# Last step of the conv FFNs in three chunks instead of four, and the order of work at the norm transitions

## What is computed

```python
def rmsnorm(x, g):
    y = xf * lax.rsqrt(jnp.mean(xf * xf, axis=-1, keepdims=True) + EPS)
    return (y * g.astype(jnp.float32)).astype(x.dtype)

def conv_gated_ffn(h, w_up, conv_w, conv_b, w_down):      # w_up 1024 x 2*2752, w_down 2752 x 1024
    u = h @ w_up
    u = lax.conv_general_dilated(u, conv_w[:, None, :], ..., feature_group_count=C) + conv_b
    gate, val = jnp.split(u, 2, axis=-1)
    return (jax.nn.silu(gate) * val) @ w_down
```

## Time and profile before

| | |
|---|---|
| median of 3 executions | 1830.35 us (1830.26 to 1830.57) |
| the profiled execution | 1831.45 us, span 1829.7 us |
| mean granted clock of TensorE | 0.992 |
| PE, matmuls | 1786.2 us, 98% of the span, 14408 instructions |
| DVE, ACT | 1248.0 us (68%), 999.3 us (55%) |
| weights read | 302.48 MB, 166 GB/s over the span; 16 DMA engines about half busy |

### The profile page before, as it was taken

How to read it: one execution, slowest core, us unless ns; L and a number is a source line. 1 busy time by engine, 2 the same in 40 slices (tenths; PEclk the granted TensorE clock), 3 DMA queues, 4 the chain that set the end, 5 groups by cost and what they waited for, 6 DMA issues and landing times.

```text
span 1829.7 us, 35759 instructions
## 1 busy us (share of the span) xinstructions
PE 1786.2 (98%) x14408; PEld 1737.5 (95%) x14408; DVE 1248.0 (68%) x1799; ACT 999.3 (55%) x1493; POOL 76.4 (4%) x125
## 2 busy tenths in 40 slices
PE   7999999999999999999999999998999999999998
PEld 6999999999999998999999999998999999989997
DVE  6667877765787776787776687786655675656554
ACT  4666555654655566655566665565444645445443
POOL 1000000011000004000000000000200010000000
PEclk8999999999999999999999999998999999999999
DMA  8344655534465545465554456554555453535552
GB/s 276 123 155 143 205 182 167 173 127 127 151 208 181 169 162 162 141 206 184 166 168 145 136 177 206 191 159 139 186 183 183 155 181 127 173 105 195 184 183 92
DMA packets 229466, 305.31 MB, mean 167 GB/s; under 512 B 4985, under 2 KB 204203, under 8 KB 229310
## 3 DMA queue, kind: packets, MB, share of 16 engines
q1 hardware_dynamic: 228150, 299.28, 50.8%
q0 software_dynamic: 1088, 4.22, 0.7%
q10 hardware_dynamic: 104, 0.07, 0.0%
HBM read 302.48 MB, written 1.07 MB: 166 GB/s over the span
## 4 chain that ended last, share of the span: by engine, by line
PE 79%; DVE 9%; ACT 7%; issue 3%; DMA 1%; ACTq 0%; DVEq 0%
PE ps L957 25%; PE ps L958 24%; PE ps L959 24%; DVE sb_w_lo L1463 4%; ACT sb_w_hi L802 3%; DVE sb_work L1814 2%; PE ps L1114 1%; DVE sb_work L1800 1%; DMA sb_raw<-in_da_w_qkv 1%; PE ps L1134 0%; ACT sb_a_hi L842 0%; ACT sb_work L912 0%; PE ps L1201 0%; DVE sb_y L1538 0%; ACT sb_hh L934 0%
## 5 line engine op out<-in xcount | busy, mean ns | idle before, releaser
L957 PE MATMUL ps<-sb_a_hi,sb_w_hi 128*128 128x256 f32 x3152 | 905.8, 287 | 20.4 <-DVE sb_w_lo L1463 10.8
L1463 DVE TENSOR_TENSOR sb_w_lo<-sb_raw,sb_w_hi 128x2048 fp32r<-128x2048 f32 x284 | 649.6, 2291 | 393.8 <-ACT sb_w_hi L802 393.7
L958 PE MATMUL ps<-sb_a_lo,sb_w_hi 128*128 128x256 f32 x3152 | 894.7, 284 | 0.0
L959 PE MATMUL ps<-sb_a_hi,sb_w_lo 128*128 128x256 f32 x3152 | 894.5, 284 | 0.0
L802 ACT ACTIVATE sb_w_hi<-sb_raw 128x2048 fp32r<-128x2048 f32 x284 | 540.0, 1906 | 290.7 <-PE ps L959 270.1
L957 PEld LDWEIGHTS ps<-sb_a_hi,sb_w_hi 128*128 128x128 f32 x3152 | 607.1, 193 | 31.9 <-DVE sb_w_lo L1463 12.4
L958 PEld LDWEIGHTS ps<-sb_a_lo,sb_w_hi 128*128 128x128 f32 x3152 | 607.3, 193 | 0.8
L959 PEld LDWEIGHTS ps<-sb_a_hi,sb_w_lo 128*128 128x128 f32 x3152 | 607.3, 193 | 0.0
L957 PE MATMUL ps<-sb_hh,sb_w_hi 128*128 128x256 f32 (+1 forms) x912 | 257.7, 283 | 4.6 <-DVE sb_w_lo L1463 3.4
L958 PE MATMUL ps<-sb_hl,sb_w_hi 128*128 128x256 f32 (+1 forms) x912 | 256.8, 282 | 0.0
L959 PE MATMUL ps<-sb_hh,sb_w_lo 128*128 128x256 f32 (+1 forms) x912 | 256.6, 281 | 0.0
(11 more groups left out here) (211 smaller groups left out, 1426.9 us busy)
## 6 DMA issues: line engine op xcount, KB each, us to landing
sb_raw<-in_ffn_w_up SPq DMA_DIRECT2D x102, 1024.0 KB, 5.3
sb_raw<-in_ffn_w_down SPq DMA_DIRECT2D x62, 1024.0 KB, 4.9
sb_raw<-in_da_w_qkv SPq DMA_DIRECT2D x24, 1024.0 KB, 5.2
sb_raw<-in_ffn_w_gate SPq DMA_DIRECT2D x22, 1024.0 KB, 5.3
sb_raw<-in_w_o SPq DMA_DIRECT2D x16, 1024.0 KB, 4.9
sb_raw<-in_sb_w_qkv SPq DMA_DIRECT2D x12, 1024.0 KB, 5.1
sb_raw<-in_xa_wkv SPq DMA_DIRECT2D x8, 1024.0 KB, 5.4
sb_raw<-in_w_in SPq DMA_DIRECT2D x8, 1024.0 KB, 5.3
```

The source lines that it names most:

```text
L957: pe.matmul(o, hi1, hi2, start=start, stop=False, skip_group_check=True)
L958: pe.matmul(o, hi1, lo2, start=False, stop=False, skip_group_check=True)
L959: return pe.matmul(o, lo1, hi2, start=False, stop=stop, skip_group_check=True)
L1463: dve.tensor_tensor(w_lo[:, a % RING, :], raw[:, a % RING, :], w_hi[:, a % RING, :].bitcast(F32), ALU.subtract).then_inc(lo_ready, 1)
```

## The change

1. **Last step of the conv FFNs** (`packed`). Chunk 0 becomes 128 gate and 128 value channels. The 64 that are left share one chunk: their gate and value columns stand side by side in one matmul, gate in PSUM partitions 0 to 63 and value in 64 to 127. The first up block holds 128 gate and 128 value columns, the second 64 and 64. Both are loaded by two DMAs each, and SP waits for the first to land before it issues the second. `take` of the second chunk is two instructions of 64 partitions; it writes partitions 64 to 127, and all later work of that chunk, the down product too, uses these (`rows`).
2. **First step** of all FFNs but the last one: part 0 slice by slice, then part 1 whole.
3. **Bridges, ACT:** w_hi of n+3 stands behind the first pair of hi copies, and the four squares of the next norm behind all hi copies.
4. **First bridge:** the sum of the memory's squares moves on DVE to the FFN before, right behind `mem_lo`; w_lo of block 34 moves behind the four additions of `finish`. On PE both `square_total`s stand together in the first block (j = 1, k = 5).

```diff
         if ph["mem_turned"]:
             stat(ph["mem_turned"])
+            ph["tree"], ph["mem_turned"]["tree"] = ph["mem_turned"]["tree"], ph["tree"]
...
+        def packed(ph, s0):
+            return s0 == NSTEP - 1 and ph["F"] == F1
+        def rows(ph, s0, c):
+            return slice(HD, P) if packed(ph, s0) and c else slice(0, P)
...
                     def up(s0, s, ph=ph):
                         for part in range(2):
...
+                            if packed(ph, s0):
+                                n, first = (P, HD)[part], 2 * P * s0 + P * part
+                                halves = [io[w][l][:, h * F1 + first:h * F1 + first + n].rearrange("(k p) n -> p k n", p=P)
+                                          for h in range(2)]
+                                wait_block(sp, b - RING)
+                                sp.dma_start(slot(b, KC)[:, :, n:2 * n], halves[1]).then_inc(s_half_in, 16)
+                                sp.wait_ge(s_half_in, 16 * (2 * ph["index"] + part + 1))
+                                load(b, s, slot(b, KC)[:, :, 0:n], halves[0])
+                                continue
...
                     for i in range(4):
-                        prep_pair(ph["then"], i)
-                    if ph["blocks"]:
-                        split(ph["n"] + 3)
+                        prep_hi(ph["then"], i)
+                        if i == 0 and ph["blocks"]:
+                            split(ph["n"] + 3)
+                    for i in range(4):
+                        square_pair(x[:, 2 * i:2 * i + 2, :], i)
...
-                            if (i, j, k) == (0, 1, 1):
+                            if (i, j, k) == (0, 1, 5 if ph["mem_turned"] else 1):
                                 square_total(ph["stat"], ph["tree"], ph["bank"])
-                            if ph["mem_turned"] and (i, j, k) == (1, 1, 3):
-                                mem = ph["mem_turned"]
-                                square_total(mem["stat"], mem["tree"], 4 + (ph["bank"] - 3) % 4, sq_mem)
+                                if ph["mem_turned"]:
+                                    mem = ph["mem_turned"]
+                                    square_total(mem["stat"], mem["tree"], 4 + (ph["bank"] - 3) % 4, sq_mem)
...
                 def up(s0, s):
                     for part in range(2):
                         wait_block(pe, up_block(ph, s0, part), s)
-                        for c in range(2):
+                        for i in range(2 * KC):
+                            first = s0 == 0 and part == 0
+                            c, k = (i % 2, i // 2) if first else (i // KC, i % KC)
...
+                            if first and c == 0:
+                                wait_slice(k)
+                            ins = up_product(s0, part, c, k)
...
+                    if s0 == 0:
+                        square_total(ph["stat"], tree_of[ph["stat"]])
+                def packed_up(s0):
+                    for part in range(2):
+                        b, u = up_block(ph, s0, part), ph["u"] + 2 * s0 + part
+                        wait_block(pe, b)
+                        pe.wait_ge(u_free, u - 3)
+                        wh, wl = weights(b, KC)
+                        for h in range(2 - part):
+                            cs = slice(h * P, (h + 1) * P)
+                            for k in range(KC):
+                                ins = product(UB[u % 4][:, h * T:(h + 1) * T], wh[:, k, cs], wl[:, k, cs],
+                                              a_hi[a][:, k, :], a_lo[a][:, k, :], k == 0 and h == 0, k == KC - 1)
...
-                first_up()
+                if ph["dst"] == "tok":
+                    both_first_ups()
+                else:
+                    up(0, 0)
...
-                if ph["mem_turned"]:
-                    dve.wait_ge(sq_mem_ready, 4)
-                    square_sum(sq_mem)
...
                     def take(c):
-                        if c == 0:
+                        if c == 0 and packed(ph, s0):
+                            dve.wait_ge(blocks_done, b + 1)
+                        elif c == 0:
                             dve.wait_ge(half_done, ph["hd"] + s0 + 1 + s)
...
+                        if packed(ph, s0) and c:
+                            ps = rows(ph, s0, c)
+                            for h in range(2):
+                                ins = dve.tensor_tensor(us[ps, c, h, :], UB[u % 4][h * HD:(h + 1) * HD, 0:T], r_all[ps, 0, :],
+                                                        ALU.mult)
...
                 def down(s0, s):
-                    if s0 < NSTEP - 1:
+                    if s0 < NSTEP - 2 or s0 == NSTEP - 2 and "mem" not in ph:
                         split(down_block(ph, s0) + 3, s)
                     if s0 == NSTEP - 3:
                         hidden_lo(NSTEP - 1, 0)
                         if "mem" in ph:
                             mem_lo(ph["mem"]["fill"])
+                            square_sum(sq_mem)
...
                 if ph["dst"] == "x":
                     chunk_pairs(ph, finish)
+                if "mem" in ph:
+                    split(down_block(ph, NSTEP - 2) + 3)
```

More of the change, by code:

```diff
@@ L503, in down @@
                     def down(s0, s, ph=ph):
-                        n = cols(ph, s0)
                         w, l = ph["down"]
                         b = down_block(ph, s0)
-                        src = io[w][l][bass.ds(2 * P * s0 + 2 * P * s, 2 * n), :]
-                        load(b, s, slot(b, 2)[0:n, :, :], src.rearrange("(k p) n -> p k n", p=n))
+                        if packed(ph, s0):
+                            row0 = io[w][l][2 * P * s0:2 * P * s0 + P, :]
+                            src = bass.AP(row0.tensor, row0.offset, [[D, P], [HD * D, 2], [1, D]])
+                            return load(b, s, slot(b, 2), src)
+                        src = io[w][l][bass.ds(2 * P * s0 + 2 * P * s, 2 * P), :]
+                        load(b, s, slot(b, 2), src.rearrange("(k p) n -> p k n", p=P))
                     ffn_steps(sp, up, down)
@@ L926, in up @@
                                 act.wait_ge(hid_ready, f - 1 + 2 * s)
-                                src = us[0:n, c, 0, :]
-                            act.activation(sil[0:n, c, :], src, ACT.Silu).then_inc(sil_ready, 1)
+                                src = us[ps, c, 0, :]
+                            act.activation(sil[ps, c, :], src, ACT.Silu).then_inc(sil_ready, 1)
                         for c in range(2):
@@ L933, in up @@
                             act.wait_ge(hid_ready, ph["f"] + 2 * s0 + c + 1 + 2 * s)
-                            act.activation(hh[0:n, 2 * (s0 % 2) + c, :], hid[0:n, c, :], ACT.Copy).then_inc(hh_ready, 1)
+                            ps = rows(ph, s0, c)
+                            act.activation(hh[ps, 2 * (s0 % 2) + c, :], hid[ps, c, :], ACT.Copy).then_inc(hh_ready, 1)
                         if s0 == 1 and ph["dst"] == "tok":
@@ L1351, in down @@
                     if ph["dst"] == "tok":
-                        return down_by_token(s0, s, n, wh, wl, last)
+                        return down_by_token(s0, s, wh, wl, last)
                     order = ([(k, m) for i in range(4) for k in range(2) for m in (2 * i, 2 * i + 1)] if last
@@ L1361, in down @@
                         first = first_down and s0 == 0 and k == 0 and m % 2 == 0
-                        ins = product(DB[m // 2][:, (m % 2) * T:(m % 2 + 1) * T], wh[0:n, k, m * P:(m + 1) * P],
-                                      wl[0:n, k, m * P:(m + 1) * P], hh[0:n, at, :], hl[0:n, at, :], first,
+                        ps, ms = rows(ph, s0, k), slice(m * P, (m + 1) * P)
+                        ins = product(DB[m // 2][:, (m % 2) * T:(m % 2 + 1) * T], wh[ps, k, ms], wl[ps, k, ms],
+                                      hh[ps, at, :], hl[ps, at, :], first,
                                       last and k == 1)
@@ L1383, in ffn @@
                         down(d + 2, PE_LSTEPS * i)
-                up(NSTEP - 1, 0)
+                if packed(ph, NSTEP - 1):
+                    packed_up(NSTEP - 1)
+                else:
+                    up(NSTEP - 1, 0)
                 for st in range(NSTEP - 3, NSTEP):
@@ L1799, in take @@
                             dve.wait_ge(hid_ready, f - 1 + 2 * s)
-                        dve.tensor_tensor(us[0:n, c, :, :], pairs(UB[u % 4])[0:n], both(r_all[0:n, 0, :]), ALU.mult)\
-                            .then_inc(u_free, 1)
+                        if packed(ph, s0) and c:
+                            ps = rows(ph, s0, c)
+                            for h in range(2):
+                                ins = dve.tensor_tensor(us[ps, c, h, :], UB[u % 4][h * HD:(h + 1) * HD, 0:T], r_all[ps, 0, :],
+                                                        ALU.mult)
+                            ins.then_inc(u_free, 1)
+                            return
```

(3 more changed lines are left out.)

63 lines of the change are left out of this document (30 added, 33 removed).

## The result

The changed kernel takes **1846.57 us** (median of 4 runs, 1845.52 to 1846.81), the kernel before 1830.3 beside it: the ratio is 1.0088, interval 1.0071 to 1.0106. It is 0.9% slower. The forecast was 1818.8, with a range up to 1823.6; what came is rival (e), priced at 1836.9 and dearer than that.

A forecast was written before the change was run, and what follows sets the result against it. PE, 98% busy, was taken to bound the kernel except where ACT and DVE set its waits. Gains 5.6 + 9.5 + 2.7 less 0.3 made 17.5 us, less 6.0 for the clock: 1818.8 us, range 1812.0 to 1823.6.

The forecast's parts named there:

- rival (e): At four new stalls and the products behind: clock low for 12 us after each, 6 us lost each, 1836.9 us; chance 0.03.
- The clock: Behind four new stalls, three before last downs and one at the first bridge: 1.5 us lost each, 6.0 in all.
- The stall, "3.4 after": Ahead of the last down in three conv FFNs: PE arrives 2.86 us sooner and waits 3.4 us instead of 0.58.
- The 0.1: Last step's take(1), split into two instructions: 0.1 us added to the chain per FFN, between ends 0.07 and 0.68.
- Part 1's matmul count gains nothing in three FFNs: Packed last step: 24 fewer matmuls (2.86 us) per FFN gain nothing there, as ACT and DVE set the last down's start.
- the waits at 186.94 and 193.80: PE's w_lo waits early in an FFN: removed by the root's chain coming 2.0 us sooner, gaining 1.4 us in each of four.
- The later bridges: Bridges after the first: w_lo of n+3 starts sooner, removing stalls of 1.30 + 0.16 and 1.12 + 0.16, 2.7 us gained.
- the 1.1 owed to part 1: Fourth FFN: the packed step starts the last down 1.1 us sooner, counted within the first bridge's gain of 9.5 us.
- The double loads: Up blocks loaded by two DMAs in the last step: costed at nothing; uncovered, one extra landing of 4.6 us per block.
- a wait of SP for these blocks: Loads of blocks 28 and 29: a wait of SP or ACT for them would show the prediction wrong.
- the 2.1 us wait for the sum of the squares: First bridge: PE waits 2.1 us for DVE's sum of squares, since w_lo 34 now stands in its path.
- the stall ahead of the last down (1.8 forecast): Fourth FFN: a new PE stall of 1.8 us before the last down, which starts 1.1 us sooner; counted with the bridge.

The follow-up runs named there:

- full_rows: Changed kernel, stall kept, with the last down multiplying all 128 rows of the second chunk, stale values in rows 0 to 63 (output differs): 1819.61 us.
- zero_stall: Changed kernel, stall kept, with the second chunk's copies and down products on all 128 rows, rows 0 to 63 holding zeros: 1819.93 us.
- parts234: Kernel before with parts 2 to 4 of the change alone, its last step left unpacked: 1810.37 us, ratio 0.9892.
- hl_first: Changed kernel with hidden_lo of step 10 moved ahead of w_lo of block 33 on DVE, 64-row products kept: 1808.56 us, ratio 0.9886.
- best1: Changed kernel with hidden_lo ahead of w_lo 33, zero-filled 128-row products, and w_lo 34 behind additions and lo pairs in all four conv FFNs: 1805.75 us.
- pack_only: Kernel before with part 1 of the change alone (packed last step), first steps and bridges as before: 1860.8 us, ratio 1.017.
- zero_rows: Changed kernel with hidden_lo ahead of w_lo 33 and the second chunk's rows 0 to 63 zero-filled, so products use 128 rows: 1812.41 us.
- stall20: Kernel before with an extra DVE instruction of about 1.9 us ahead of hidden_lo of step 10 in the first three conv FFNs: 1839.52 us.

## Why the prediction was wrong

**The step that failed is "The clock".** It said: "3.4 is nearest to 3.87, and I take 1.5: 4 x 1.5 = 6.0 us lost". The rows it drew on the earlier trace rows are stalls followed by 128-row products only, and this one is followed by products of which half have 64 rows. The low stretch lasted 17.07 us in all four FFNs, not 3.4. For 16.96 of them PE was at work in the first FFN, and a matmul every 0.213 us instead of every 0.119 loses 0.44 of that: 7.5 us each, some 30 in all instead of 6. full_rows and zero_stall against the changed kernel show it: the same stall, other row counts, 27 us less. Rival (e) had the place and the mechanism, with a low clock of 12 us and a chance of 0.03; nothing in it asked what the products behind the stall were. The four places were not quite the ones named either: the bridge's stall didn't come, the one in the fourth FFN did.

Two smaller steps of the account, each read off the first FFN against parts234, where a last down takes 5.77:

- **The stall, "3.4 after".** 4.19 idle, 4.35 by the prediction's count, as the chain grew by 0.97 us, not 0.1. The 0.1, with its ends of 0.07 and 0.68, was for take(1) alone, and that grew by 0.29, between the ends. The other 0.68, in the taps, w_lo 32, the hidden copies and ahead of take(1), was not in the sum.
- **Not in the sum: the changes of row count.** The last down is 6.81 us longer: 48 x 0.094 = 4.5 by the half clock, so 2.3 for eight changes. At full clock (hl_first) seven cost 1.3.

The rest of the low stretch, 4.38 us, loses about 2.0. Together 0.97 + 6.81 + 2.0 = 9.8 us per FFN, in three of them 29.3, and 7.9 in the fourth with its bridge (from norm total to norm total 213.4 us for 205.5 in parts234): 37.2, against 37.3 between the two spans. The 7.5 that the clock costs are in it: 4.5 + 2.0, and 1.0 of the changes, which are dearer at half clock.

**Right:**

- Part 1's matmul count gains nothing in three FFNs, since ACT and DVE set the start of the last down, and the wait goes to hidden_lo. hl_first shows it from the other side: off that chain, the last down starts 20.03 us behind the step's start instead of 23.41.
- Part 2: the waits at 186.94 and 193.80 are gone; 1.8 us for each first step where 1.4 was forecast. The root's chain is 2.15 us earlier behind the total (parts234), where 2.0 was forecast.
- The later bridges: 1.55 and 1.37 us for 1.46 and 1.28.
- Parts 2 to 4 together: 16.7 by the terms (17.8 less the 1.1 owed to part 1), 20.0 measured.
- The double loads: no wait of PE or ACT is for one. SP waits eight times for a first half, 24.5 us in all, beside 1598 us of waiting for free slots. The prediction had named a wait of SP for these blocks as a sign of being wrong; it is there and holds nothing up.

**Half right:** at the first bridge the 2.1 us wait for the sum of the squares. In the changed kernel it isn't there, as PE comes late and at half clock; in parts234 it is 0.48; in hl_first and best1, where PE is on time, it is 2.5 and 3.8. In the fourth FFN the stall ahead of the last down (1.8 forecast) was 2.36 us:

```profile
1241.73 0.36 PE L982 MATMUL ps<-sb_hh,sb_w_hi 128*128 128x256 f32 x1 [2.36 <-DVE sb_hl L1897]
```

and it was this one that the prediction should have counted as a fifth chance for the clock, beside the bridge's. It fell, for 17.07 us. In full_rows the same stall left the clock at 1.00, in zero_stall it did not: a toss again.

The Trainium skill, TensorE: Matmul & The Clock Gate, section HAM oscillation, says that groups of matmuls with waits between them can pay the low clock at each wait anew. The trace agrees for the three stalls of 4.2 us in each kernel that has them. That the row count sets how long it lasts is what these runs add.

**Open:** why stalls of 2.1 to 2.5 us bring the clock down in some places and not in others; why the low stretch behind one and the same stall of 3.87 us is 3.41 us in some kernels and 6.83 in others; and whether it is the rows or another property of a 64-row product (its place in rows 64 to 127, say) that keeps the clock low, since a product on rows 0 to 63 wasn't tried.

## What to carry to other kernels

When an edit takes matmuls away, ask whether PE then waits, and what PE does right behind that wait: products on few rows can hold the low clock for as long as they last and beyond, so that a stall of 4 us costs 7.5 more here, and 1.5 with products of 128 rows. Long stalls and thin products are each cheap alone and dear together. Break the pair at its cheaper end, here by moving one pair of DVE instructions ahead of a wait (38.0 us), or fill the rows with zeros so that all products use 128 (26.6). And price a low clock only from a stretch whose products have the shape of those that will stand there.

## What was unexpected of the hardware

- Length of the low stretch that goes with a stall, by the rows of the products behind it: 3.41 us with 128 (stalls of 4.18 to 4.26) and 3.41 or 6.83 (3.87), 3.41 or 6.83 with 96 (3.69), 10.24 with 24 products of 64 first (4.64), 17.07 with 64 and 128 in turn (4.19, and once behind 2.36; once 13.65, behind 2.41 in pack_only). Rows of zeros count as rows.
- At 1.00 already, 64-row products don't bring the clock down (hl_first).
- A change between 128 and 64 rows costs about 0.19 us at full clock (0.21 and 0.22 for two steps of 0.12), and about 0.3 at half clock (0.35 and 0.38 for two of 0.21).
- The clock can fall behind 2.18 us of idle time (zero_rows) and hold behind 2.22 (stall20) and 2.47 (hl_first).
